# Retention's queries and its normalised output transposed by VectorE and GpSimd in place of TensorE

## The chip, the cores and the metric

The kernel runs on one core of a Trainium2 chip. The metric is the device time of one execution in microseconds. The engines are TensorE (PE in the rows; PEld is its weight load), VectorE (DVE), ScalarE (ACT), GpSimd (POOL) and SyncE (SP). Each works through its own queue in order, and they wait for one another on semaphores.

## The reference

Two blocks of layers on 256 tokens of width 1024, all in fp32: a SwiGLU feed-forward part, token mixing, a second feed-forward part, then a recurrent mixer and a short-convolution mixer. The change is in token mixing, and there in the retention branch (4 heads, queries and keys of 128, values of 256):

```python
rq, rk, rv, rg, nq, nk, nv, g_ret, g_na = jnp.split(u @ w_in, points, axis=-1)
q = _rotary(heads(rq, RET_QK_DIM), pos)
k = _rotary(heads(rk, RET_QK_DIM), pos) * (RET_QK_DIM ** -0.5)
y = _bidirectional_retention(q, k, heads(rv, RET_V_DIM), decay_fwd, decay_bwd)
y = y * lax.rsqrt(jnp.mean(y * y, axis=-1, keepdims=True) + RMS_EPS)
y_ret = (jax.nn.silu(rg) * y) @ w_ret_out
y_na = _neighborhood_attention(na_heads(nq), na_heads(nk), na_heads(nv), rel_bias) @ w_na_out
merged = jax.nn.sigmoid(g_ret) * y_ret + jax.nn.sigmoid(g_na) * y_na
return merged @ w_out
```

## The kernel before

Weights come as groups of 128x2048 numbers (1 MB) through a ring of six slots. SyncE asks for a group (L406) when TensorE has done with the group six before it. ScalarE rounds a group to its high part w_hi (L525, `round_to`), VectorE takes the rest as w_lo (L979, `low_to`), and a product of two fp32 matrices becomes three products of parts (L1610 to L1612). Activations are split in the same way and have to lie transposed, with the inner dimension on the partitions.

The mixing stage's input product goes by column blocks c = 0 to 12 and halves t = 0, 1 of the tokens. A step is called a slot: slot = 2c + t. Each engine has a loop over the slots, and after the product of a slot TensorE does small work from elsewhere (`extras`): in the slots 7 to 24 neighbourhood attention, where unit s has its scores in slot 7 + s, the transpose of its probabilities one slot later (L1828, waiting for VectorE's scaling L1232) and the product with the values two slots later (L1838). Retention runs between:

- slots 2 and 3: VectorE's `rotate` of rq, whose two parts GpSimd adds in `stage` (L489); slots 8 and 9 the same for rk;
- slots 6 and 7: TensorE transposes rq out of `stage` into PSUM (L1796), and VectorE copies it to rqT (L1197); slots 10 and 11 the same for rk;
- slots 12 to 15: scores of retention; slots 18 to 21: their product with the values, multiplied into the gate in y_ret (L1321);
- slot 22: ScalarE's root (L766), then VectorE's reciprocal and eight scalings of y_ret (L1331); behind these, at the head of slot 23, the scaling of the last unit's probabilities (L1231, L1232);
- slots 24 and 25: TensorE transposes y_ret (L1796), ScalarE takes the high part yretT_hi (L535) and VectorE the low part yretT_lo (L1007).

GpSimd also adds the mask to the attention biases (`mask_bias`, L479), a unit ahead of need at most two, each behind VectorE's reduction of an earlier unit, and loads them (L448). Then come the output products: na_out (2 groups) into acc, ret_out (4 groups) into aux, the merge on VectorE (L1344, L1353, L1355), mix_out. In the queues of ScalarE and VectorE the roundings of ret_out's groups 1 to 3 and of mix_out's first stand behind slot 25.

In the two feed-forward stages the hidden values are already transposed without TensorE: VectorE turns 32x32 blocks (L1139), and GpSimd carries the blocks between groups of 32 partitions with sixteen transfers for each pair of tiles (L459, `move_tiles`).

Of the kernel before, what the change touches and what calls it, by code (L numbers as in the profile page):

```python
# [63 lines left out]
for _name in ACC_READERS:  # L64
# [3 lines left out]
FILL_COUNTS = [("t1", 4), ("rq", 2), ("rk", 2), ("rs", 4), ("rp", 4),  # L68
               ("yret", 4), ("merged", 4), ("t2", 4), ("t3", 4),
# [3 lines left out]
SPLIT_COUNTS = [("t1", 4), ("yret", 4), ("merged", 4), ("t2", 4), ("t3", 4), ("gate", 6), ("t4", 4), ("b_in", 12)]  # L73
# [51 lines left out]
def build(nc, first_in, weights, x_turned_in, x_in, gain0_in, gains, rot_in, colmask_in, dist_in, decay_in, lam_in, bias_in, gate_w_in,  # L125
          gate_b_in, conv_a_in, conv_ab_in, conv_b_in, out):
    with ExitStack() as ctx:
# [77 lines left out]
        yretT_lo = at("yretT_lo", [P, KD, S], F32R, area + 24576)  # L205
        rqT = at("rqT", [P, RH, S], F32, area + 16384)
        rkT = at("rkT", [P, RH, S], F32, area + 20480)
        m_ret = at("m_ret", [P, T, DM], F32, area + 16384)
# [111 lines left out]
        y_ret_ready = sem("y_ret_ready")  # L320
        ret_acc_full = sem("ret_acc_full")
# [97 lines left out]
        def _(pool):  # L419
# [52 lines left out]

            def mask_bias(s):
                pool.wait_ge(bias_in_s[s % 2], 16 * (s // 2 + 1))
                if s == 0:
                    pool.wait_ge(consts_in, 16 * 8)
                if s >= 2:
                    pool.wait_ge(s_reduced, s - 1)
                g.tensor_tensor(bias_m[:, s % 2], bias_raw[:, s % 2],  # L479
                                colmask[:, KINDS[s % NB]].unsqueeze(1).to_broadcast([P, GR, KB]), ALU.add).then_inc(bias_ready, 1)  # L480
                if s + 2 < UNITS:
                    load_bias(s + 2)
# [3 lines left out]
            for n in range(2 * T):  # L486
                t = n % T
                pool.wait_ge(acc_free_dve[t], ACC_ORDER[:FIRST_ACC["mix_in"] + (2, 5)[n // T]].count("V"))
                g.tensor_tensor(stage[:, t], stage[:, t], rot_b[:, t], ALU.add).then_inc(rot_done, 1)  # L489
                if n:  # L490
                    mask_bias(n + 1)
            for s in range(2 * T + 1, UNITS):
                mask_bias(s)
            pool.wait_ge(bank_full, FIRST_FILL["rp"] + RH)
            load_gains(2, 3, 4)
            pool.wait_ge(xn_ready, 12)
# [20 lines left out]
        def _(act):  # L517
# [208 lines left out]
            for c in range(13):  # L726
                for t in range(T):
# [40 lines left out]
                    if slot in (24, 25):  # L768
                        tt = slot - 24
                        for h in range(2):  # L770
                            bank = h
                            take_hi("yret", 2 * tt + h, yretT_hi[:, 4 * h:4 * h + 4, tt * P:(tt + 1) * P], bank,
                                    source=aux[:, bank].rearrange("p (c q) -> p c q", c=4))
# [197 lines left out]
        def _(dve):  # L971
# [243 lines left out]
            for c in range(13):  # L1215
                for t in range(T):
# [21 lines left out]
                    if slot in (3, 8, 9):  # L1238
                        dve.wait_ge(acc_full[t], c0 + c + 1)
                        if c == 4:  # L1240
                            dve.wait_ge(bank_full, FIRST_FILL["rq"] + t + 1)
                        rotate(t, par, T * (c // 4) + t)
# [34 lines left out]
                    if slot in (6, 7, 10, 11):  # L1277
                        name, dst = ("rq", rqT) if slot < 10 else ("rk", rkT)
                        copy_fill(name, t, [(dst[:, :, t * P:(t + 1) * P], heads_of(0))])
# [53 lines left out]
                    if slot in (24, 25):  # L1333
                        tt = slot - 24
                        cols = slice(tt * P, (tt + 1) * P)
                        for h in range(2):
                            chunks = slice(4 * h, 4 * h + 4)
                            take_lo("yret", 2 * tt + h, yretT_lo[:, chunks, cols], yretT_hi[:, chunks, cols],
                                    heads_of(h))
            low_to(FIRST_GROUP["ret_out"] + 4)  # L1340
            for t in range(T):
                dve.wait_ge(acc_full[t], FIRST_ACC["na_out"] + 1)
                dve.wait_ge(acc_free_act[t], ACC_ORDER[:FIRST_ACC["na_out"]].count("A"))
                v.scalar_tensor_tensor(m_na[:, t], m_na[:, t], 1.0, acc[:, t].rearrange("p h n -> p (h n)"),  # L1344
                                       ALU.add, ALU.mult).then_inc(acc_free_dve[t], 1)
# [257 lines left out]
        def _(pe):  # L1603
# [237 lines left out]
            def extras(slot):  # L1841
                if slot in (6, 7, 10, 11):
                    t = slot % 2
                    n = slot - 6 if slot < 10 else slot - 8
                    pe.wait_ge(rot_done, n + 1)
                    transposes(0, stage[:, t], FIRST_FILL["rq"] + n)
                if 12 <= slot < 16:
                    h = slot - 12
                    pe.wait_ge(bank_free, FIRST_FILL["rs"] + h)
                    for k in range(T):  # L1850
# [25 lines left out]
                if slot in (24, 25):  # L1876
                    t = slot - 24
                    pe.wait_ge(y_ret_ready, t + 1)
                    for h in range(2):
                        transposes(h, y_ret[:, t, h * 512:(h + 1) * 512],  # L1880
                                   FIRST_FILL["yret"] + 2 * t)
# [33 lines left out]
            pe.wait_ge(bank_free, FIRST_FILL["yret"] + 4)  # L1915
            for t in range(T):
                for n in range(4):
# [229 lines left out]
```

## Time and profile before

| | us |
|---|---|
| median of 3 runs | 883.44 (883.14 to 883.91) |
| the profiled execution | 883.76 |
| its span | 882.0 |
| TensorE busy | 873.6 |
| VectorE busy | 602.2 |
| ScalarE busy | 461.9 |
| GpSimd busy | 174.5 |

The span runs from the first instruction to the last; the rest of an execution's time lies around it. Starts are microseconds from the span's start. TensorE's instructions are pipelined: the distance between two starts tells what one costs, the duration is longer. The mixing stage's slots lie from about 200 to 354, na_out begins at 354.49 and ret_out at 365.75.

### The profile page before, as it was taken

How to read it: one execution, taken by the hardware profiler on the slowest of the kernel's cores; microseconds unless marked ns; L12 is line 12 of the kernel's file. 1: busy time of each engine (PE TensorE's matmuls, PEld its weight loads, DVE VectorE, ACT ScalarE, POOL GpSimd, SP SyncE). 2: the span in 40 equal slices, each digit the busy share in tenths (PEclk: the TensorE clock that was granted, in tenths of full speed). 3: DMA queues.
4: the chain of work that ended last, by engine and by line, in shares of the span. 5: the costliest groups of instructions: out<-in, count | busy, mean ns of one | idle time of the engine just before them, and what ended most of it. 6: DMA issues, size and time to landing. Idle time of an engine off the chain costs nothing.

```text
span 882.0 us, 10831 instructions
## 1 busy us (share of the span) xinstructions
PE 873.6 (99%) x4320; PEld 737.3 (84%) x4320; DVE 602.2 (68%) x720; ACT 461.9 (52%) x570; POOL 174.5 (20%) x281
## 2 busy tenths in 40 slices
PE   9999999999999999999999999999999999999997
PEld 7788888888888888888888888888999888888886
DVE  6757666468767656577666667446979857888872
ACT  6645454455444556446444445445886644555551
POOL 2544452003021110000244445000480000000000
PEclk9999999999999999999999999999999999999999
DMA  9976665456653444455666666556434456555521
GB/s 348 367 232 228 215 219 211 143 191 203 260 202 133 172 174 171 185 191 190 246 216 216 215 216 224 192 203 247 162 128 159 169 187 241 191 191 191 191 96 48
DMA packets 33089, 175.62 MB, mean 199 GB/s; under 512 B 6688, under 2 KB 7248, under 8 KB 14096
## 3 DMA queue, kind: packets, MB, share of 16 engines
q1 hardware_dynamic: 24368, 161.23, 50.4%
q0 software_dynamic: 8384, 13.44, 5.1%
q8 instruction: 34, 0.56, 0.3%
q10 hardware_dynamic: 288, 0.27, 0.1%
q14 instruction: 15, 0.12, 0.0%
HBM read 167.05 MB, written 1.05 MB: 191 GB/s over the span
## 4 chain that ended last, share of the span: by engine, by line
PE 94%; DVE 2%; ACT 2%; DMA 1%; SPq 1%; issue 0%; ACTq 0%; DVEq 0%
PE acc L1610 22%; PE acc L1612 22%; PE acc L1611 22%; PE acc L2025 8%; PE acc L2027 4%; PE acc L1807 2%; PE acc L1977 2%; PE acc L1978 2%; PE acc L1976 2%; DMA raw<-weights 1%; DVE w_lo L979 1%; PE aux L1961 1%; PE aux L1728 1%; PE acc L1809 1%; PE aux L1611 1%; PE aux L1610 1%
## 5 line engine op out<-in xcount | busy, mean ns | idle before, releaser
L979 DVE TENSOR_TENSOR w_lo<-raw,w_hi 128x2048 fp32r<-128x2048 f32 x147 | 337.2, 2301 | 119.8 <-ACT w_hi L525 119.4
L525 ACT ACTIVATE w_hi<-raw 128x2048 fp32r<-128x2048 f32 x145 | 276.1, 1913 | 58.9 <-DMA raw<-weights 58.7
L1610 PE MATMUL acc<-w_hi,xT 128*128 128x512 f32 x600 | 236.2, 394 | 0.6 <-DVE w_lo L979 0.6
L1612 PE MATMUL acc<-w_hi,xT 128*128 128x512 f32 x600 | 233.8, 390 | 0.0
L1611 PE MATMUL acc<-w_lo,xT 128*128 128x512 f32 x600 | 233.6, 389 | 0.0
L459 POOL DMA_DIRECT2D hT_raw<-turned x192 | 109.6, 579 | 122.0 <-DVE turned L1139 120.3
L1610 PEld LDWEIGHTS acc<-w_hi,xT 128*128 128x128 f32 x600 | 112.7, 188 | 24.4 <-DVE w_lo L979 1.0
L1612 PEld LDWEIGHTS acc<-w_hi,xT 128*128 128x128 f32 x600 | 112.6, 188 | 23.8
L1611 PEld LDWEIGHTS acc<-w_lo,xT 128*128 128x128 f32 x600 | 112.7, 188 | 22.6
L2025 PE MATMUL acc<-xT,w_hi 128*128 128x512 f32 x320 | 111.3, 394 | 0.0
L2027 PE MATMUL acc<-xT,w_lo 128*128 128x256 f32 x320 | 88.7, 277 | 0.0
L2025 PEld LDWEIGHTS acc<-xT,w_hi 128*128 128x128 f32 x320 | 60.0, 188 | 13.8
L1610 PE MATMUL acc<-w_hi,hT_hi 128*128 128x512 f32 x176 | 68.6, 390 | 0.0
L1612 PE MATMUL acc<-w_hi,hT_lo 128*128 128x512 f32 x176 | 68.5, 389 | 0.0
L1611 PE MATMUL acc<-w_lo,hT_hi 128*128 128x512 f32 x176 | 68.5, 389 | 0.0
L2027 PEld LDWEIGHTS acc<-xT,w_lo 128*128 128x128 f32 x320 | 60.1, 188 | 0.0
L1128 DVE TENSOR_TENSOR prod<-acc,silu_g 128x256 f32<-128x256 f32 x44 | 18.6, 423 | 40.6 <-ACT silu_g L651 22.8
L651 ACT ACTIVATE silu_g<-acc 128x256 f32<-128x256 f32 x22 | 8.5, 385 | 60.5 <-PE acc L1612 60.0
L1612 PEld LDWEIGHTS acc<-w_hi,hT_lo 128*128 128x128 f32 x176 | 33.0, 188 | 6.9
L1611 PEld LDWEIGHTS acc<-w_lo,hT_hi 128*128 128x128 f32 x176 | 33.0, 188 | 6.8
L1610 PEld LDWEIGHTS acc<-w_hi,hT_hi 128*128 128x128 f32 x176 | 33.0, 188 | 6.8
L1610 PE MATMUL acc<-w_hi,yT_hi 128*128 128x512 f32 x96 | 37.5, 390 | 0.0
(244 smaller groups left out, 1144.3 us busy)
## 6 DMA issues: line engine op xcount, KB each, us to landing
raw<-weights SPq DMA_DIRECT2D x147, 1024.0 KB, 4.8
hT_raw<-turned POOLq DMA_DIRECT2D x160, 32.0 KB, 2.7
gain_pre<-gains POOLq DMA_DIRECT2D x5, 512.0 KB, 5.2
raw<-weights SPq DMA_DIRECT2D x4, 512.0 KB, 7.9
gain_post<-gains POOLq DMA_DIRECT2D x3, 512.0 KB, 5.9
gate_w<-gate_w_in POOLq DMA_DIRECT2D x1, 1536.0 KB, 9.1
x_turned<-x_turned_in SPq DMA_DIRECT2D x4, 256.0 KB, 5.1
x<-x_in SPq DMA_DIRECT2D x2, 512.0 KB, 12.1
```

The lines of the kernel that those rows point to most:

```text
L459: pool.dma_start(hT_raw[quad, chunks[0]:chunks[1], :, i, :].rearrange("p c t b -> p (c t) b"), turned[32 * i:32 * i + 32, p % 2, 0:n, :, q, :]
L525: a.activation(w_hi[:, g % RING], raw[:, g % RING], ACT.Copy).then_inc(hi_done, 1)
L979: v.tensor_tensor(w_lo[:, slot], raw[:, slot], w_hi[:, slot].bitcast(F32), ALU.subtract)\
L1128: v.tensor_tensor(prod[:, par, :, t], acc[:, t, par, 256:512].rearrange("p (c n) -> p c n", c=2), silu_g[:, t].rearrange("p (c n) -> p c n ...
L1610: m.matmul(dst, hi[:, k, cols], w_hi[:, slot, w], start=first, stop=False)
L1611: m.matmul(dst, hi[:, k, cols], w_lo[:, slot, w], start=False, stop=False)
L1612: return m.matmul(dst, lo[:, k, cols], w_hi[:, slot, w], start=False, stop=last)
L1807: m.matmul(dst, w_hi[:, g % RING, w], xT[:, k].rearrange("p a q -> p (a q)"), start=k == 0, stop=False)
L1976: m.matmul(dst, w_hi[:, slot, w], xT_hi[:, k, :], start=k == 0, stop=False)
L1977: m.matmul(dst, w_hi[:, slot, w], xT_lo[:, k, :], start=False, stop=False)
L2025: m.matmul(dst, w_hi[:, g % RING, w], xT[:, k].rearrange("p a q -> p (a q)"), start=k == 0, stop=False)
L2027: i = m.matmul(dst[:, 0:S], w_lo[:, g % RING, w], xT[:, k, 0], start=False, stop=k == KD - 1)
```

## The change

rq and y_ret are no longer transposed on TensorE. For each, VectorE turns the 32x32 blocks in place of the transposes (two instructions for rq in slots 4 and 5, two of 128x1024 for y_ret in slot 22), and GpSimd moves the blocks across partitions with sixteen transfers each (32 KB each for rq, 64 KB each for y_ret). rq lands in rqT directly; y_ret lands in yr_moved, from where ScalarE takes the high part and VectorE the low part, in two instructions of 128x1024 each, after slot 25. VectorE waits for rq's moves in slot 10 (rk's tile lies where rq_turned lay), TensorE in slot 12. TensorE's wait ahead of ret_out is for yretT_lo, one half of the tokens at a time. The declarations of the new semaphores are left out here.

```diff
@@ FILL_COUNTS, SPLIT_COUNTS
-FILL_COUNTS = [("t1", 4), ("rq", 2), ("rk", 2), ("rs", 4), ("rp", 4),
-               ("yret", 4), ("merged", 4), ("t2", 4), ("t3", 4),
+FILL_COUNTS = [("t1", 4), ("rk", 2), ("rs", 4), ("rp", 4),
+               ("merged", 4), ("t2", 4), ("t3", 4),
...
-SPLIT_COUNTS = [("t1", 4), ("yret", 4), ("merged", 4), ("t2", 4), ("t3", 4), ("gate", 6), ("t4", 4), ("b_in", 12)]
+SPLIT_COUNTS = [("t1", 4), ("merged", 4), ("t2", 4), ("t3", 4), ("gate", 6), ("t4", 4), ("b_in", 12)]
@@ tiles
+        yr_turned = at("yr_turned", [P, KD, T, QUADS, 32], F32, area + 53248)
+        yr_moved = at("yr_moved", [P, KD, T, QUADS, 32], F32, area + 24576)
+        rq_turned = at("rq_turned", [P, RH, T, QUADS, 32], F32, area + 20480)
+        rq_moved = rqT[:].rearrange("p h (t i b) -> p h t i b", t=T, b=32)
@@ GpSimd
+            def move_blocks(dst, src, done):
+
+                for i in range(QUADS):
+                    for q in range(QUADS):
+                        pool.dma_start(dst[32 * q:32 * q + 32, :, :, i, :].rearrange("p c t b -> p (c t) b"),
+                                       src[32 * i:32 * i + 32, :, :, q, :].rearrange("p c t b -> p (c t) b"))\
+                            .then_inc(done, 16)
...
                 if n:
                     mask_bias(n + 1)
+                if n == 1:
+                    pool.wait_ge(rq_tiles_turned, T)
+                    move_blocks(rq_moved, rq_turned, rq_landed)
             for s in range(2 * T + 1, UNITS):
                 mask_bias(s)
             pool.wait_ge(bank_full, FIRST_FILL["rp"] + RH)
             load_gains(2, 3, 4)
+            pool.wait_ge(yr_tiles_turned, T)
+            move_blocks(yr_moved, yr_turned, yr_landed)
@@ ScalarE
-                    if slot in (24, 25):
-                        tt = slot - 24
-                        for h in range(2):
-                            bank = h
-                            take_hi("yret", 2 * tt + h, yretT_hi[:, 4 * h:4 * h + 4, tt * P:(tt + 1) * P], bank,
-                                    source=aux[:, bank].rearrange("p (c q) -> p c q", c=4))
+            act.wait_ge(yr_landed, 16 * MOVES)
+            for t in range(T):
+                a.activation(yretT_hi[:, :, t * P:(t + 1) * P], yr_moved[:, :, t].rearrange("p c i b -> p c (i b)"),
+                             ACT.Copy).then_inc(yr_hi, 1)
             round_to(FIRST_GROUP["mix_out"] + 1)
@@ VectorE
-                        if c == 4:
-                            dve.wait_ge(bank_full, FIRST_FILL["rq"] + t + 1)
                         rotate(t, par, T * (c // 4) + t)
...
-                    if slot in (6, 7, 10, 11):
-                        name, dst = ("rq", rqT) if slot < 10 else ("rk", rkT)
-                        copy_fill(name, t, [(dst[:, :, t * P:(t + 1) * P], heads_of(0))])
+                    if slot in (4, 5):
+                        dve.wait_ge(rot_done, t + 1)
+                        v.transpose(rq_turned[:, :, t].rearrange("p c q b -> p c (q b)"),
+                                    stage[:, t].rearrange("p (c n) -> p c n", c=RH)).then_inc(rq_tiles_turned, 1)
+                    if slot in (10, 11):
+                        if t == 0:
+                            dve.wait_ge(rq_landed, 16 * MOVES)
+                        copy_fill("rk", t, [(rkT[:, :, t * P:(t + 1) * P], heads_of(0))])
...
                             i.then_inc(y_ret_ready, 1)
-                    if slot in (24, 25):
-                        tt = slot - 24
-                        cols = slice(tt * P, (tt + 1) * P)
-                        for h in range(2):
-                            chunks = slice(4 * h, 4 * h + 4)
-                            take_lo("yret", 2 * tt + h, yretT_lo[:, chunks, cols], yretT_hi[:, chunks, cols],
-                                    heads_of(h))
+                        for tt in range(T):
+                            dve.wait_ge(y_ret_ready, tt + 1)
+                            v.transpose(yr_turned[:, :, tt].rearrange("p c q b -> p c (q b)"),
+                                        y_ret[:, tt].rearrange("p (c n) -> p c n", c=KD)).then_inc(yr_tiles_turned, 1)
             low_to(FIRST_GROUP["ret_out"] + 4)
+            for t in range(T):
+                dve.wait_ge(yr_hi, t + 1)
+                cols = slice(t * P, (t + 1) * P)
+                v.tensor_tensor(yretT_lo[:, :, cols], yr_moved[:, :, t].rearrange("p c i b -> p c (i b)"),
+                                yretT_hi[:, :, cols].bitcast(F32), ALU.subtract).then_inc(yr_lo, 1)
@@ TensorE
-                if slot in (6, 7, 10, 11):
+                if slot in (10, 11):
                     t = slot % 2
-                    n = slot - 6 if slot < 10 else slot - 8
-                    pe.wait_ge(rot_done, n + 1)
-                    transposes(0, stage[:, t], FIRST_FILL["rq"] + n)
+                    pe.wait_ge(rot_done, T + t + 1)
+                    transposes(0, stage[:, t], FIRST_FILL["rk"] + t)
                 if 12 <= slot < 16:
                     h = slot - 12
                     pe.wait_ge(bank_free, FIRST_FILL["rs"] + h)
+                    if h == 0:
+                        pe.wait_ge(rq_landed, 16 * MOVES)
...
-                if slot in (24, 25):
-                    t = slot - 24
-                    pe.wait_ge(y_ret_ready, t + 1)
-                    for h in range(2):
-                        transposes(h, y_ret[:, t, h * 512:(h + 1) * 512],
-                                   FIRST_FILL["yret"] + 2 * t)
...
-            pe.wait_ge(bank_free, FIRST_FILL["yret"] + 4)
             for t in range(T):
+                pe.wait_ge(yr_lo, t + 1)
                 for n in range(4):
                     out_tile("ret_out", n, t, yretT_hi, yretT_lo, KD, aux_target, lambda t: (ret_acc_full, 1))
```

## Rows read from the trace of the kernel before

**Rows 1.** The page's busy time, share of the span and instructions of each engine.
```profile
PE 873.6 (99%) x4320; PEld 737.3 (84%) x4320; DVE 602.2 (68%) x720; ACT 461.9 (52%) x570; POOL 174.5 (20%) x281
```

**Rows 2.** The page's chain that ended last: shares of the span by engine.
```profile
PE 94%; DVE 2%; ACT 2%; DMA 1%; SPq 1%; issue 0%; ACTq 0%; DVEq 0%
```

**Rows 3.** Timeline of TensorE, slot 7: start, duration, engine, line, operation, out<-in, shape, count.
```profile
234.61 0.60 PE L1796 MATMUL aux<-ident,stage 128*128 128x128 f32 x4
235.05 0.39 PE L1821 MATMUL aux<-nkT,nqT 128*128 128x128 f32 x2
```

**Rows 4.** Timeline of TensorE from slot 23 to the start of ret_out.
```profile
341.21 0.33 PE L1828 MATMUL aux<-ident,prob 128*128 128x128 f32 x1
341.38 0.39 PE L1838 MATMUL aux<-probT,nv_b 128*128 128x128 f32 x2
341.52 0.48 PE L1610 MATMUL acc<-w_hi,xT 128*128 128x512 f32 x1
...
347.11 0.39 PE L1838 MATMUL aux<-probT,nv_b 128*128 128x128 f32 x2
...
348.12 0.47 PE L1610 MATMUL acc<-w_hi,xT 128*128 128x512 f32 x1
...
353.69 1.04 PE L1796 MATMUL aux<-ident,y_ret 128*128 128x128 f32 x8
354.49 0.47 PE L1610 MATMUL acc<-w_hi,ynaT_hi 128*128 128x512 f32 x1
...
365.75 0.40 PE L1610 MATMUL aux<-w_hi,yretT_hi 128*128 128x512 f32 x1
```

**Rows 5.** Timeline of VectorE, end of slot 22 and head of slot 23.
```profile
338.57 2.19 DVE L1331 TENSOR_SCALAR y_ret<-y_ret,ret_rstd 128x256 f32<-128x256 f32 x8
340.68 0.16 DVE L1231 RECIPROCAL prob_rec<-prob_sum 128x1 f32<-128x1 f32 x1
```

**Rows 6.** The feed-forward turns, whole span: durations in ns min/median/max, first and last start.
```profile
L1139 DVE STREAM_TRANSPOSE turned<-prod x22: 711/711/715, 28.9 to 534.1; 128x512 f32<-128x512 f32 x22
```

**Rows 7.** Feed-forward moves: turn before, two sets of sixteen, a weight request, two moves.
```profile
117.95 0.71 DVE L1139 STREAM_TRANSPOSE turned<-prod 128x512 f32<-128x512 f32 x1
...
L459 POOL DMA_DIRECT2D hT_raw<-turned x16: 584/584/584, 119.0 to 127.6; - x16
...
DMA to landing us min/median/max: 1.8/2.3/5.7
...
L459 POOL DMA_DIRECT2D hT_raw<-turned x16: 551/551/562, 129.8 to 138.0; - x16
...
125.06 0.33 SPq L406 DMA_DIRECT2D raw<-weights  x1
...
L459 POOL DMA_DIRECT2D hT_raw<-turned x2: 584/584/584, 124.7 to 125.3; - x2
...
DMA to landing us min/median/max: 3.1/4.1/5.2
```

**Rows 8.** Timelines of ScalarE and VectorE from the last slot to ret_out.
```profile
353.89 0.60 ACT L748 ACTIVATE m_na<-acc 128x512 f32<-128x512 f32 x1 [2.42 <-PE acc L1612]
354.39 1.08 ACT L535 ACTIVATE yretT_hi<-aux 128x512 fp32r<-128x512 f32 x2
355.34 5.53 ACT L525 ACTIVATE w_hi<-raw 128x2048 fp32r<-128x2048 f32 x3
...
357.31 6.70 DVE L979 TENSOR_TENSOR w_lo<-raw,w_hi 128x2048 fp32r<-128x2048 f32 x3 [1.00 <-ACT w_hi L525]
363.92 1.21 DVE L1344 SCALAR_TENSOR_TENSOR m_na<-m_na,acc 128x1024 f32<-128x1024 f32 x1
```

**Rows 9.** Timeline of SyncE's requests, last tile of the mixing input.
```profile
351.16 0.33 SPq L406 DMA_DIRECT2D raw<-weights  x1
```

**Rows 10.** Timelines of GpSimd and VectorE, slots 7 and 10.
```profile
236.93 0.46 POOL L479 TENSOR_TENSOR bias_m<-bias_raw,colmask 128x128 f32<-128x128 f32 x1 [19.68 <-DVE neg_max L1291]
...
254.75 0.68 DVE L1197 COPY rkT<-aux 128x512 f32<-128x512 f32 x1
```

More of the change, by code:

```diff
@@ L320, in build @@
         y_ret_ready = sem("y_ret_ready")
+        rq_tiles_turned, rq_landed = sem("rq_tiles_turned"), sem("rq_landed")
+        yr_tiles_turned, yr_landed = sem("yr_tiles_turned"), sem("yr_landed")
+        yr_hi, yr_lo = sem("yr_hi"), sem("yr_lo")
         ret_acc_full = sem("ret_acc_full")
```

## The prediction, made before the changed kernel was built

> **What bounds the kernel now.** I read the busy times first: TensorE is busy for 873.6 of 882.0 us [rows 1]. Then the chain of waits: 94% of the span is TensorE's own work [rows 2]. So time is won where TensorE loses instructions, and lost wherever it is made to wait; an engine with slack matters only at the place where TensorE asks for its result. Next I read TensorE's timeline at the transposes that go away [rows 3, 4], to price them by the distance between the starts of neighbouring instructions (one instruction's own duration overlaps the next). Then VectorE's timeline just before TensorE's wait in slot 23 [rows 5], because there the trace shows no slack at all: TensorE's transpose of the last probabilities starts at 341.21, 0.05 us after VectorE has scaled them (340.68, 0.53 us earlier, is where VectorE begins on that). Last, the moves that POOL already does in the feed-forward stages, as the model for the new ones [rows 7], and the run-up to ret_out [rows 8].
>
> **Removed from TensorE.** Four transposes for rq take 0.44 us (234.61 to 235.05), twice [rows 3]. In slot 24 the next tile starts 1.01 us after the last attend product (347.11 to 348.12); in slot 23, which has no y_ret transposes, 0.14 us (341.38 to 341.52): 0.87 us. In slot 25 eight transposes put 0.80 us ahead of na_out (353.69 to 354.49) [rows 4]. Sum: 0.44 + 0.44 + 0.87 + 0.80 = **2.55 us**, all on TensorE's path. If nothing else came of it, the time would fall by that.
>
> **rq's new way, costed at nothing.** VectorE turns stage in slots 4 and 5 (0.71 us each [rows 6]) and saves the two rqT copies out of PSUM in slots 6 and 7. POOL reaches the sixteen moves only after mask_bias(2), which waits for the first score reduction and starts at 236.93 [rows 10]. Behind them in POOL's queue stand the addition for rk, mask_bias(3) and the bias load after it. One move has 32 KB, as in the feed-forward stages, where sixteen are issued in 9.2 us; from about 238 they are issued by 247 and, with the worst landing there (5.7 us [rows 7]), in place by 253. VectorE waits for them just before its copy of rk at 254.75 [rows 10], and TensorE two slots later. The rk addition of slot 8 is held to 247 but is needed in slot 10, some 6 us later. The cover is thus about 2 us at the worst; beyond it every microsecond of lateness holds VectorE in slot 10 and the attention chain after it.
>
> **Slot 23: a wait in place of the transposes.** The two transposes of y_ret come right behind the normalisation in VectorE's queue (L1331, 338.57), ahead of the scaling of the last probabilities (340.68) [rows 5]. No row has a transpose of 128x1024. The 128x512 one takes 0.711 us [rows 6]; the bounds are that number and its double, 0.71 to 1.42. A 128x1024 operation of another kind takes 1.21 us (L1344) [rows 8], so I take 1.25 us, and 2.50 for the two. Queued behind them are the scaling, w_lo of na_out and the copy of probT; TensorE waits for the scaling alone. Having had no slack, it waits **2.50 us**. Call E the end of these transposes, 340.68 + 2.50 = 343.18 on the old clock (the 0.88 us won earlier left out). This alone takes back what was removed.
>
> **The run-up to ret_out.** TensorE's side, with E as zero and steps from [rows 4]: the transpose in slot 23 at 0.53, first product of the next tile 0.31 later (341.21 to 341.52), that tile 5.59 (to 347.11), 0.14 to the last tile, that tile 5.57 (348.12 to 353.69): na_out starts at E + 12.14. na_out takes 11.26 us (354.49 to 365.75): TensorE is free for ret_out at **E + 23.40**.
>
> The data's side. ScalarE finishes m_na 0.70 us after the last tile (353.69 to 354.39) [rows 4, 8]: E + 12.84. If the moves have landed, it makes yretT_hi, twice as large per instruction as the 128x512 pair that took 0.95 us (354.39 to 355.34): 1.90 for both. Only then come the roundings of ret_out's groups 1 to 3, and in VectorE's queue their w_lo stand ahead of yretT_lo: 1.97 from the first rounding to the first w_lo (355.34 to 357.31), 6.61 for three (to 363.92), 1.21 for the first yretT_lo by L1344's row [rows 8]. That is 11.69 us from the start of yretT_hi, so ret_out could start at E + 24.53. TensorE waits **1.13 us even if the moves come in time**. Here the old kernel had the split of y_ret done by slot 25; now it is late next, with three w_lo ahead of it. Behind yretT_lo in VectorE's queue m_na and the merge wait, but they need ret_out's first result, 11 us on.
>
> When do the moves land? POOL starts them 0.3 us after VectorE's transpose (117.95 + 0.71 against 119.0) [rows 7]. Sixteen of 256 blocks of 128 bytes are spread over 8.6 us (119.0 to 127.6), 0.576 apart; of 128 blocks over 8.2, 0.545 apart [rows 7]. The new ones have 512 blocks each. By that slope they are 0.64 us apart (estimate), within bounds of 0.576 and, if time went with the blocks, 1.15. The last is then issued at E + 0.3 + 15 x 0.64 = E + 9.9. Without company a move lands in 1.8 us. But a weight group was asked for at 125.06, and the move issued at 125.3 took 5.2 us instead [rows 7]. Here SyncE asks for a group 3.04 us into the last tile (348.12 to 351.16) [rows 4, 9], which will be E + 6.57 + 3.04 = E + 9.61. The last move comes 0.3 us behind it, as in the row, and lands at E + 15.1. ScalarE, free since E + 12.84, starts 2.26 us late, and so does ret_out: TensorE waits 1.13 + 2.26 = **3.39 us**.
>
> The Trainium skill (DMA: Bandwidth & Descriptors, "Queues, rings and completion order") says that each DMA engine takes turns between its queues packet by packet. By that a move need not wait for a whole weight group; the rows disagree, 5.2 us against 1.8, and I go by the rows.
>
> **Sum.** -2.55 + 2.50 + 3.39 = +3.34 us. After ret_out's start all transfers and waits follow TensorE, so the shift stays. The profiled execution took 883.76 us (span 882.0): 887.1. The median of the runs is 0.3 us lower, so I say **886.8 us**.
>
> **Rivals.**
> First, the moves miss the weight group: not slower. If 512 blocks cost no more issue time than 256, the last move is issued at E + 8.9, 0.7 us ahead of the request; the row with 1.8 us shows such moves landing at once. It decides at a spacing of about 0.60 us. Then only the 1.13 us remain: -2.55 + 2.50 + 1.13 = +1.08, 884.5 us. For it: the margin is a third of a microsecond. Against it: spacing does grow with the blocks. The Trainium skill's rule of turns would give the same time even behind the group.
>
> Second, POOL is the bound: at 1.15 us apart the last move is issued at E + 17.5 and lands at E + 19.3; ret_out starts at E + 31.0, a wait of 7.6 us, 891.0 us in all. At 0.8 apart the moves run into the next weight group too, which gives about 889.7. Against it: a doubling of blocks cost 6% before.
>
> Third, everything is hidden: neither wait comes, and 2.55 us are won, 880.9 us. It needs VectorE to reach the probabilities in slot 23 in time, against the order in its queue, and transposes far below 0.7 us.
>
> Fourth, VectorE keeps POOL from writing its moves. If each cost six times its 0.576 us, the last would be issued near E + 52 and the time would rise by over 35 us, to about 920. Against it: in the feed-forward stages the sixteen keep their spacing while VectorE works beside them [rows 7]. The Trainium skill (SBUF — State Buffer) warns that VectorE's fast fp32 copies lock GpSimd out of a shared port, so that such transfers wait for their descriptors; here no such copy runs in that stretch, and no row shows the wait.
>
> **How the numbers follow.** Forecast 0.50, first rival 0.25, second 0.14, third 0.09, fourth 0.02. The range takes in the first rival, the forecast with the bounds of the transposes (1.1 down, 0.3 up) and of the landing (5.7 for 5.2), and the milder half of the second: 883.6 to 889.8 us. A measurement of this kernel can tell 0.2%, 1.8 us, from no change. Faster by more than that needs the third rival: 0.09. Within it lies the first, with a little from the forecast's lower edge: 0.26. Slower: 0.65.
>
> **What would show it.** Right: in slot 23 TensorE idle for 2.5 us until VectorE's scaling; two transposes of about 1.25 us ahead of it; sixteen moves some 0.64 us apart, the last landing 5 us after issue; ScalarE idle on them; TensorE idle for over 3 us at ret_out until VectorE's yretT_lo; no new wait at slots 10 and 12. Wrong: a first idle much shorter, because the transposes are cheaper; moves all landed before ScalarE asks (884.5); or moves a microsecond apart (891). A wait on rq's moves in slot 10 would be an addition that I don't expect.

## The result, and the profile after

Median of nine runs: 888.60 us (885.48 to 890.08), beside 883.51 us (883.14 to 883.91) for nine runs of the kernel before. The ratio, which is near that of the means (the medians alone give 1.0058), is 1.0047, with a 95% interval of 1.0034 to 1.0060: slower by about half a per cent. The nine times fall in two groups, four from 885.48 to 886.13 us and five from 888.60 to 890.08 us, with nothing between. The profiled execution is of the upper group: it took 888.88 us, its span is 887.1 us (before: 882.0), and all rows of this section are its own.

The page's first rows (span; busy time of each engine, share and instructions; the chain that ended last, by engine) answer [rows 1] and [rows 2].

```profile
span 887.1 us, 10809 instructions
PE 872.7 (98%) x4296; PEld 736.1 (83%) x4296; DVE 606.1 (68%) x720; ACT 462.0 (52%) x568; POOL 195.4 (22%) x313
PE 89%; DVE 3%; ACT 3%; DMA 2%; POOL 1%; issue 1%; SPq 1%; DVEq 0%; ACTq 0%
```

TensorE has 24 instructions fewer, as the diff says, yet its busy time fell by only 0.9 us, and its share of the chain fell from 94% to 89%: for some stretch that chain now runs through other engines. The timelines say where. VectorE at the end of slot 22 and TensorE in slot 23 (start, duration, engine, line, operation, out<-in, count, and in brackets the idle time before it and what ended that), against [rows 4] and [rows 5]:

```profile
337.46 2.19 DVE L1352 TENSOR_SCALAR y_ret<-y_ret,ret_rstd 128x256 f32<-128x256 f32 x8
339.57 2.36 DVE L1356 STREAM_TRANSPOSE yr_turned<-y_ret 128x1024 f32<-128x1024 f32 x2
341.86 0.12 DVE L1249 RECIPROCAL prob_rec<-prob_sum 128x1 f32<-128x1 f32 x1
...
342.35 0.33 PE L1851 MATMUL aux<-ident,prob 128*128 128x128 f32 x1 [2.20 <-DVE prob L1250]
```

The two transposes hold VectorE from 339.57 to 341.86, 2.29 us, and TensorE idles for 2.20 us until the scaling behind them. Next the stretch up to ret_out, as the chain of waits tells it (start, time, what):

```profile
339.65 2.29 DVE yr_turned L1356 x2
...
342.22 9.68 POOL yr_moved L484 x15
351.91 5.71 DMA yr_moved<-yr_turned
...
357.64 2.01 ACT yretT_hi L790 x2
359.65 1.81 ACT w_hi L545
...
361.49 3.65 DVE w_lo L997 x2
...
365.90 2.28 DVE w_lo L997
368.18 1.15 DVE yretT_lo L1362
```

This is one unbroken path through four engines: the turn, the moves one by one, the landing of the last, ScalarE's two halves, and then three w_lo ahead of yretT_lo. In [rows 8] yretT_hi began at 354.39, straight after m_na; here it begins at 357.64. Where the lateness of the moves sets in is told by the answer on the two issued just ahead of SyncE's request of 351.42:

```profile
L484 POOL DMA_DIRECT2D yr_moved<-yr_turned x2: 651/651/651, 350.6 to 351.3; - x2
...
DMA to landing us min/median/max: 2.1/4.0/5.9
```

The one issued 0.8 us ahead of the request landed in 2.1 us, the one issued 0.16 us ahead in 5.9. That one (at 357.1) and the last move (at 357.6) landed about when the weight group itself did, 5.9 us after its request (at 357.3).

TensorE's side of it, and the windows around it (columns: stretch and its length, then busy time and instructions of PE, PEld, DVE, ACT and POOL, granted clock, DMA share, GB/s):

```profile
351.42 0.33 SPq L413 DMA_DIRECT2D raw<-weights  x1
...
369.37 0.80 PE L1633 MATMUL aux<-w_hi,yretT_hi 128*128 128x512 f32 x1 [4.07 <-DVE yretT_lo L1362]
...
372.48 0.40 PE L1634 MATMUL aux<-w_lo,yretT_hi 128*128 128x512 f32 x1
```

```profile
365.20:369.30 4.10, 0.10 (x1) 0.00 (x0) 4.10 (x4) 1.91 (x1) 0.00 (x0) 0.96 0.96 372
369.30:372.40 3.10, 3.03 (x7) 2.46 (x8) 3.07 (x4) 0.00 (x0) 0.00 (x0) 0.50 0.05 21
372.40:376.00 3.60, 3.60 (x17) 2.96 (x17) 0.44 (x1) 0.00 (x0) 0.00 (x0) 1.00 0.00 0
```

TensorE idles for 4.07 us ahead of ret_out, and its granted clock then stands at 0.50, the lower of its two levels (1.2 GHz), until 372.4. Seven products take 3.11 us there (369.37 to 372.48); seven of the same line take 1.60 us at 1.00 (experiment weights_first, below: 366.95 to 368.55). That is 1.5 us more.

The account of this execution, in spans: -2.55 (instructions gone, as priced) + 2.20 (slot 23) + 4.07 (ret_out) + 1.5 (half clock after it) = +5.2 us; measured 887.1 - 882.0 = +5.1.

### The profile page after: what moved, and what is told of

It reads as the page before. It is cut to its first block, busy times and chain, and to the rows that moved or that the text cites. A ratio compares the mean times of both kernels' runs of the same rounds, so it can differ in the third digit from the quotient of the medians.

```text
span 887.1 us, 10809 instructions
## 1 busy us (share of the span) xinstructions
PE 872.7 (98%) x4296; PEld 736.1 (83%) x4296; DVE 606.1 (68%) x720; ACT 462.0 (52%) x568; POOL 195.4 (22%) x313
## 3 DMA queue, kind: packets, MB, share of 16 engines
HBM read 167.05 MB, written 1.05 MB: 189 GB/s over the span
## 4 chain that ended last, share of the span: by engine, by line
PE 89%; DVE 3%; ACT 3%; DMA 2%; POOL 1%; issue 1%; SPq 1%; DVEq 0%; ACTq 0%
PE acc L1633 21%; PE acc L1635 21%; PE acc L1634 21%; PE acc L2043 8%; PE acc L2045 4%; PE acc L1830 2%; DVE w_lo L997 2%; PE acc L1995 2%; PE acc L1996 2%; PE acc L1994 2%; DMA raw<-weights 1%; POOL yr_moved L484 1%; PE aux L1979 1%; PE aux L1633 1%; PE aux L1635 1%; PE aux L1634 1%
```

## The experiments

My theory: the removed instructions are worth their 2.55 us, and what is lost comes from two places in in-order queues, y_ret's transposes ahead of VectorE's scaling (slot 23) and the wait for the moves ahead of three roundings and splits (ret_out). The rivals were that the moves as such are too late, that the two waits add up independently, that the lateness isn't due to the weight request, and that a wait costs TensorE its length and no more. "Before" is the median of the kernel before in the same session.

**Weights first.** ScalarE rounds all groups of ret_out ahead of its wait for the moves:

```
+            round_to(FIRST_GROUP["ret_out"] + 4)
             act.wait_ge(yr_landed, 16 * MOVES)
```

> The changed kernel with one order altered: ScalarE rounds ret_out's groups 1 to 3 ahead of its wait for y_ret's moves, so that behind the moves only one high part and one low part stand (0.95 + 1.2 us instead of 11.7). Theory (ret_out is held by moves that land behind a weight group, and then by the three w_lo queued ahead of yretT_lo): TensorE's 4.07 us of idle time before ret_out shrinks below 1 us, the granted clock no longer falls there, slot 23 keeps its 2.2 us; the time comes to about the time of the kernel before, 883 to 884 us. Rival (the moves themselves are too late): idle of at least 2 us stays before ret_out and the time stays above 885.5.

Measured: 884.47 us (882.88 to 885.35, 11 runs) against 883.44; ratio 1.0008, interval 0.9999 to 1.0017. The timeline of TensorE has no idle time left ahead of ret_out, while the wait in slot 23 is unchanged:

```profile
342.59 0.33 PE L1852 MATMUL aux<-ident,prob 128*128 128x128 f32 x1 [2.20 <-DVE prob L1251]
...
366.72 0.39 PE L1636 MATMUL acc<-w_hi,ynaT_lo 128*128 128x512 f32 x1
366.95 0.40 PE L1634 MATMUL aux<-w_hi,yretT_hi 128*128 128x512 f32 x1
...
368.55 0.39 PE L1635 MATMUL aux<-w_lo,yretT_hi 128*128 128x512 f32 x1
```

```profile
342.00:346.00 4.00, 3.41 (x11) 2.77 (x12) 3.96 (x6) 0.93 (x1) 3.54 (x6) 0.64 0.84 295
```

So the moves were early enough for ret_out; it was the order behind them that was late, three splits in front of yretT_lo. (In this execution SyncE's request came only at 353.23, behind the last move, and no move took over 3.1 us; last_group_after, below, has late moves and no wait either.) The window shows what I had not looked for: in this execution the granted clock fell already after slot 23's wait (a mean of 0.64 from 342 to 346, where the profile of the changed kernel has 1.00). The sum is -2.55 + 2.20 = -0.35 without that fall (883.1 us) and some 1.5 us more with it (884.6). The eleven times agree: four from 882.9 to 883.8 us, each with a granted clock of 0.999 in the mean of the whole execution, and seven from 884.3 to 885.4 us at 0.997 or 0.998.

**Probabilities first.** VectorE does the transposes in slot 23, behind the scaling that TensorE waits for, not in slot 22 ahead of it:

```
                             .then_inc(p_scaled, 1)
+                    if slot == 23:
+                        for tt in range(T):
+                            dve.wait_ge(y_ret_ready, tt + 1)
+                            v.transpose(yr_turned[:, :, tt]..., y_ret[:, tt]...).then_inc(yr_tiles_turned, 1)
```

> The changed kernel with one order altered: VectorE scales the last probabilities in slot 23 before it turns y_ret, so the wait in slot 23 goes. Theory (the chain from the turns over the moves sets ret_out's start, so the wait in slot 23 only comes out of a later one): slot 23's idle time of 2.2 us vanishes, TensorE asks for the weight groups 2 us earlier against the moves, the last of them land behind the second group, and the idle time before ret_out grows to 6 or 7 us: 888 to 890 us, no gain. Rival (the two waits add, as the sum had them): the time falls by 2.2 us against the changed kernel, to 886 or less.

Measured: 891.76 us (891.16 to 891.90, 4 runs) against 883.44; ratio 1.0092, interval 1.0079 to 1.0106. One wait is gone and the kernel is 3 us slower than with it. The answer on the sixteen moves, TensorE's timeline, and a window:

```profile
DMA to landing us min/median/max: 2.2/2.7/7.3
```

```profile
371.02 0.80 PE L1634 MATMUL aux<-w_hi,yretT_hi 128*128 128x512 f32 x1 [8.27 <-DVE yretT_lo L1363]
```

```profile
366.00:376.00 10.00, 4.98 (x12) 3.96 (x13) 8.46 (x6) 2.50 (x2) 0.00 (x0) 0.50 0.09 36
```

Without the wait TensorE reaches the tiles sooner, so SyncE asks for two weight groups before the moves are through (348.86 and 351.58), the last move lands 7.3 us after its issue, and TensorE idles for 8.27 us at ret_out. The whole window from 366 to 376 has the lower clock; the twelve products from 371.02 on take 5.29 us there instead of 12 x 0.23 = 2.8. Sum: -2.55 + 8.27 + 2.5 = +8.2; measured +7.9 in spans. The waits don't add up: what TensorE doesn't lose in slot 23 it loses at ret_out, and more. I expected 888 to 890; the idle time and the clock were both larger than I had them.

**Both orders.** The two edits together.

> Both alterations together: probabilities before the turns in slot 23, roundings before the wait for the moves. Theory: neither wait is left, what remains is the 2.55 us of removed transposes with at most 1 us of wait before ret_out: 881 to 882 us, faster than the kernel before. Rival (removed transposes are worth less than their spacing, or moves behind the second weight group still hold ret_out): 883 us or more.

Measured: 884.46 us (882.92 to 885.51, 11 runs) against 883.44; ratio 1.0008, interval 1.0000 to 1.0017. I had expected 881 to 882: a miss by 2.5 us or more. Slot 23 has no wait, but ret_out has one again, for another reason. First the timelines of SyncE, ScalarE, VectorE and TensorE, then the answer on the landing of that request:

```profile
351.24 0.33 SPq L413 DMA_DIRECT2D raw<-weights  x1
...
359.44 1.92 ACT L545 ACTIVATE w_hi<-raw 128x2048 fp32r<-128x2048 f32 x1 [2.99 <-DMA raw<-weights]
361.38 2.29 DVE L998 TENSOR_TENSOR w_lo<-raw,w_hi 128x2048 fp32r<-128x2048 f32 x1 [2.61 <-ACT w_hi L545]
...
364.87 0.50 PE L1635 MATMUL aux<-w_hi,yretT_hi 128*128 128x512 f32 x1 [2.46 <-DVE yretT_lo L1364]
```

```profile
DMA to landing us min/median/max: 8.2/8.2/8.2
```

The group asked for at 351.24 shares its time with the moves and lands 8.2 us later; ScalarE waits 2.99 us for it, and since all groups now stand ahead of yretT_hi, the late group holds what TensorE needs first. The delay goes both ways: the moves are late behind a group, and a group is late among the moves (in weights_first two groups, asked for 2.7 us apart like these but with all moves landed, took about 4.7 us each).

The profiled execution is the shortest of the eleven, 882.92 us. Its granted clock stays at 1.00 behind the wait of 2.46 us (364 to 370), and -2.55 + 2.46 = -0.1; its span, 0.8 us below that of before, is shorter still. Five of the eleven took 882.9 to 883.6 us at a mean clock of 0.999; six took 884.5 to 885.5 us, five of them at 0.996 or 0.997. A fall of the clock would account for the six, but none of them has a profile.

**The last group behind.** Both orders, but ScalarE rounds only up to ret_out's third group ahead of its wait, and VectorE's split of the fourth stands behind yretT_lo:

```
+            round_to(FIRST_GROUP["ret_out"] + 3)
             act.wait_ge(yr_landed, 16 * MOVES)
...
-            low_to(FIRST_GROUP["ret_out"] + 4)
+            low_to(FIRST_GROUP["ret_out"] + 3)
             for t in range(T):
                 dve.wait_ge(yr_hi, t + 1)
...
+            low_to(FIRST_GROUP["ret_out"] + 4)
```

> The two alterations together, and one more: ret_out's last weight group, which TensorE needs some 8 us after ret_out's start, is rounded by ScalarE behind yretT_hi and split by VectorE behind yretT_lo; the two groups before it stay ahead. Theory (what still held ret_out in the run with both orders was the last group, landed 8.2 us after its request and standing ahead of yretT_lo): the idle time of 2.46 us before ret_out goes, no fall of the granted clock is left in the mixing stage, and the 2.55 us of removed transposes show: 880.5 to 881.5 us in every run. Rival (the moves, which landed as late as 7.8 us after issue, are late by themselves): at least 1 us of idle time stays and some runs lose to the clock, 882.5 us or more.

Measured: 881.03 us (880.54 to 881.60, 9 runs) against 883.51; ratio 0.9973, interval 0.9963 to 0.9982. It beats both kernels, by 2.48 us the one before: the 2.55 us of the removed instructions, with both waits gone. The timelines of ScalarE, VectorE and TensorE, and the window behind slot 23:

```profile
360.03 2.01 ACT L791 ACTIVATE yretT_hi<-yr_moved 128x1024 fp32r<-128x1024 f32 x2 [2.67 <-DMA yr_moved<-yr_turned]
361.13 2.36 DVE L1364 TENSOR_TENSOR yretT_lo<-yr_moved,yretT_hi 128x1024 fp32r<-128x1024 f32 x2 [1.44 <-ACT yretT_hi L791]
363.88 2.29 DVE L998 TENSOR_TENSOR w_lo<-raw,w_hi 128x2048 fp32r<-128x2048 f32 x1 [0.39 <-ACT w_hi L545]
...
362.98 0.39 PE L1638 MATMUL acc<-w_hi,ynaT_lo 128*128 128x512 f32 x1
363.21 0.40 PE L1636 MATMUL aux<-w_hi,yretT_hi 128*128 128x512 f32 x1
```

```profile
342.00:346.00 4.00, 4.00 (x19) 3.31 (x18) 4.00 (x4) 1.04 (x1) 3.05 (x5) 1.00 0.84 294
```

The moves still land late (ScalarE waits 2.67 us for them), but now the wait stands where it holds nothing that TensorE asks for: ret_out follows na_out without a gap (362.98, 363.21).

**The request held back.** SyncE asks for ret_out's third group only when the moves have landed:

```
+                if g == FIRST_GROUP["ret_out"] + 2:
+                    sp.wait_ge(yr_landed, 16 * MOVES)
```

> The changed kernel, with SyncE's request for ret_out's third weight group held until y_ret's moves have landed. Theory (the runs near 888.8 us are those in which the last moves land behind that group): every move lands within about 3 us, the idle time before ret_out shrinks from 4.07 to about 2 us, and no run is near 888.8; all lie between 884 and 886.5 us. Rival (the two groups of times have another cause, such as the granted clock alone): runs near 888.8 us remain in about half of the cases.

Measured: 885.49 us (884.39 to 886.40, 11 runs) against 883.51; ratio 1.0020, interval 1.0011 to 1.0029. The answer on the moves (count, duration in ns, first and last issue, landing), and TensorE's timeline:

```profile
L486 POOL DMA_DIRECT2D yr_moved<-yr_turned x16: 648/650/691, 342.2 to 351.8; - x16
...
DMA to landing us min/median/max: 2.1/2.5/3.2
```

```profile
367.90 0.50 PE L1635 MATMUL aux<-w_hi,yretT_hi 128*128 128x512 f32 x1 [1.05 <-DVE yretT_lo L1364]
```

With the issue unchanged (about 0.65 us apart) the longest landing is 3.2 us instead of 5.7, the wait at ret_out 1.05 us instead of 4.07, and no run is near the upper group of the changed kernel. The profile alone doesn't decide it: in this execution the granted clock fell in slot 23 (a mean of 0.70 from 342 to 346), and that by itself makes the request late, as again_1 shows below. The times do: none of eleven is above 886.4 us, where five of nine were at 888.6 or more, and the four shortest (884.4 to 884.8) are near what -2.55 + 2.20 + 1.05 = +0.7 gives with no fall of the clock, 884.2. The group of weights asked for beside the moves is the cause of their lateness.

**The changed kernel again, three times.** Single profiles, to see what sets the two groups of times apart.

> The changed kernel as it is, to see a profile of each of its two groups of times. Theory: if the time is near 888.8 us, as in the first profile, the granted clock falls only after the wait ahead of ret_out and the last moves land over 5 us after issue; if it is near 886 us, the clock falls after the wait in slot 23, TensorE then asks for the weight group more than 1 us later, all moves land within about 3 us and the wait ahead of ret_out is about 1 us. Rival: the two groups differ in something else, and both show the late landing.

> The same kernel once more, with the same two expectations: late landing and a wait of about 4 us ahead of ret_out near 888.8 us; a fall of the clock in slot 23, landings within 3 us and a wait of about 1 us near 886 us.

> The same kernel a third time, with the same two expectations: late landing and a wait of about 4 us ahead of ret_out near 888.8 us; a fall of the clock in slot 23, landings within 3 us and a wait of about 1 us near 886 us.

Measured: 886.65, 890.50 and 889.47 us (before: 883.17). The first belongs with the lower group, though 0.5 us above its longest. Its timelines (slot 23, SyncE's request, ret_out), the window behind slot 23, and the answer on the moves:

```profile
342.85 0.37 PE L1851 MATMUL aux<-ident,prob 128*128 128x128 f32 x1 [2.19 <-DVE prob L1250]
...
353.50 0.33 SPq L413 DMA_DIRECT2D raw<-weights  x1
...
368.43 0.50 PE L1633 MATMUL aux<-w_hi,yretT_hi 128*128 128x512 f32 x1 [1.05 <-DVE yretT_lo L1362]
```

```profile
342.00:346.00 4.00, 3.15 (x9) 2.58 (x10) 3.96 (x6) 1.20 (x1) 3.28 (x6) 0.62 0.89 313
```

```profile
DMA to landing us min/median/max: 2.1/2.3/3.1
```

After slot 23's wait the granted clock fell. TensorE took some 1.6 us longer for the tile behind it (its slot 23 stands 0.50 us later than in the first profile, its request 2.08 us later), so SyncE's request came when the last move was already issued: landing 3.1 us at most, a wait of 1.05 us at ret_out, and no second fall. The two of the upper group had the request at 351.62 and 351.10, landings of 5.9 and 5.7 us, waits of 4.16 and 3.81 us, and the lower clock behind ret_out. The execution in which TensorE ran slower behind slot 23 took 2.8 to 3.9 us less than these two.

**Idle time alone.** In the kernel before, TensorE waits ahead of ret_out for an empty step of VectorE behind m_na, in the second version behind two more operations of 128x1024 (their results unused):

```
+            for n in range(0):      # second version: range(2)
+                step(v.scalar_tensor_tensor(rot_b[:]..., x[:, 1], 1.0, x[:, 1], ALU.add, ALU.mult))
+            dve.wait_ge(acc_free_dve[1], ...)
+            v.memset(spare2[:], 0.0).then_inc(idle_over, 1)
...
+            pe.wait_ge(idle_over, 1)
```

> The kernel before, with TensorE made to wait ahead of ret_out until VectorE has finished m_na's second half: about 1.6 us of idle time and nothing else. Theory (idle time costs its length, and beyond a certain length also a fall of the granted clock): about 885.0 us, granted clock unchanged at 1.00 around 370 us. Rival (any idle time brings the clock down): 886.4 us or more.

> The same with two more operations of VectorE of some 1.25 us each in front of TensorE: about 4.1 us of idle time, as long as the changed kernel's wait ahead of ret_out. Theory: 4.1 us and a fall of the granted clock to half for some 3 us after TensorE resumes, worth 1.5 us: about 889.0 us. Rival (the lower clock belongs to the changed kernel's other work, not to the idle time): 887.5 us, granted clock 1.00.

Measured: 885.12 us (884.48 to 885.36, 10 runs; ratio 1.0018, interval 1.0009 to 1.0027) and 890.24 us (889.40 to 890.44, 4 runs; ratio 1.0075, interval 1.0061 to 1.0088), against 883.51. TensorE's timeline and a window, of the first:

```profile
366.90 0.47 PE L1617 MATMUL aux<-w_hi,yretT_hi 128*128 128x512 f32 x1 [1.49 <-issue]
```

```profile
370.00:373.00 3.00, 3.00 (x15) 2.49 (x14) 0.00 (x0) 0.00 (x0) 0.00 (x0) 1.00 0.00 0
```

and the same two views of the second:

```profile
369.36 0.77 PE L1617 MATMUL aux<-w_hi,yretT_hi 128*128 128x512 f32 x1 [3.88 <-issue]
```

```profile
370.00:373.00 3.00, 3.00 (x9) 2.35 (x8) 0.00 (x0) 0.00 (x0) 0.00 (x0) 0.50 0.02 5
```

1.49 us of idle time cost 1.6; 3.88 us cost 6.7, 2.8 more than its length: at half clock nine products were done from 370 to 373 instead of fifteen. I had 889.0 for the second, with the clock's share too small. Nothing here moves data or changes an order of transfers, so a wait does cost TensorE more than its length.

**rq alone.** Only rq's part of the diff on the kernel before (the turn in slots 4 and 5, POOL's moves, the two waits; rq's transposes out of slots 6 and 7).

> Only rq goes the new way; y_ret is transposed by TensorE as before. Theory: two groups of four transposes leave TensorE's path and nothing takes their place: 0.9 us less than the kernel before, 882.6 us. Rival (the rq moves disturb the weight stream or VectorE in slot 10): no gain or a loss, 883.5 us or more.

Measured: 882.75 us (882.38 to 882.91, 11 runs) against 883.44; ratio 0.9991, interval 0.9982 to 1.0000. The answer on the moves, and VectorE's timeline at its copy of rk:

```profile
L480 POOL DMA_DIRECT2D rqT<-rq_turned x16: 582/582/609, 237.1 to 245.8; - x16
...
DMA to landing us min/median/max: 1.8/2.2/6.1
```

```profile
254.65 0.68 DVE L1211 COPY rkT<-aux 128x512 f32<-128x512 f32 x1
```

The last move is in place by 252 at the latest (245.8 + 6.1) and the copy starts without a wait. VectorE did not get it for nothing, though:

```profile
250.23 1.40 DVE L1246 TENSOR_SCALAR prob<-prob,prob_rec 128x128 f32<-128x128 f32 x1
```

GpSimd's two additions for rk are held up by the moves. The first (from 246.36) now falls beside a w_lo, and the addition takes 2.54 us instead of 1.28, the w_lo 3.31 instead of 2.29; the second (from 250.22) falls beside this scaling, which took 0.29 us before. VectorE's idle time ahead of the next w_lo went from 1.32 us to 0.21. It had that much slack, so TensorE did not wait.

The median is 0.69 us lower; two groups of transposes were priced at 0.88.

## Why the prediction was right, and where it was not

**Removed from TensorE: 2.55 us.** Right. last_group_after, where both waits are gone, is 2.48 us faster than before, and rq_only shows its share.

**rq at nothing.** Right for TensorE: no wait at VectorE's copy of rk, with some 2.6 us of cover (254.65 against 252) where I had about 2. That GpSimd's late additions would lengthen VectorE's operations by some 2 us in all was not on my list; VectorE's slack took it up (rq_only).

**Slot 23: 2.50 us.** Right in place and cause; the size was 2.20, since one transpose of 128x1024 takes 1.15 us and not 1.25.

**Ret_out: 3.39 us, of which 2.26 from the late moves.** The steps came out as worked, with E, the end of the transposes, at 341.86:

| step | predicted | measured |
|---|---|---|
| distance of moves | 0.64 us | 0.65 us |
| last move issued | E + 9.9 | 351.91: E + 10.05 |
| SyncE's request | E + 9.61 | 351.42: E + 9.56 |
| last move landed | E + 15.1 | 357.62: E + 15.76 |
| yretT_hi to ret_out | 11.69 us | 357.64 to 369.37: 11.73 us |
| TensorE free | E + 23.40 | 369.37 - 4.07 = 365.30: E + 23.44 |
| wait | 3.39 us | 4.07 us |

The mis-sized term is the landing: 5.7 us, where I took the 5.2 of one row. (The other 0.15 us is the issue, E + 10.05 for E + 9.9.) [rows 7] has 5.7 as its longest, and I used that only as the bound. The Trainium skill (DMA: Bandwidth & Descriptors, "Queues, rings and completion order") has each DMA engine take turns between its queues packet by packet. These runs don't show the moves gaining by that: they took 5.7 us beside a 1 MB group and landed about when it did, and 3.2 us at the longest when the group's request was held back.

**Left out: the clock.** This is the step that failed. The sum counted each wait of TensorE at its length; -2.55 + 2.20 + 4.07 gives +3.7, and the profile has +5.1. The 1.4 us between them are the products at half clock behind ret_out's wait (1.5 us, above), and idle_long shows the same with nothing else changed. Such a term could not be worked out from the rows of before that I had read, but a bound for it should have been there, since both waits were forecast; I put it at nothing without a reason. The Trainium skill (TensorE: Matmul & The Clock Gate, "Part 1: The HAM clock gate") says that the chip lowers TensorE's clock by how busy it has been of late; the rows agree (0.50 behind the wait, 1.00 from 372.4 on).

**One value for two.** The forecast of 886.8 us lies in the gap between the two groups. That it is near both is in part luck: the clock was not in the sum, and had one of the five upper runs fallen into the lower group, the median would have been about 886. The upper group is the forecast's mechanism plus the clock: 888.6 to 890.1. The lower group has the first rival's mechanism (the moves miss the weight group; the wait at ret_out is 1.05 us, where I gave 1.13), but for a reason I did not have: the clock falls in slot 23 and delays the request past the last move. -2.55 + 2.20 + 1.6 + 1.05 = +2.3, about 885.8 us; measured 885.5 to 886.1. (again_1 itself, at 886.65, stood 0.50 us later than the first profile before either wait.) My 884.5 for that rival lacked the clock again; hold_request, with the moves clear of the group, had times from 884.4 on.

**The other rivals.** POOL as the bound is out (0.65 us apart, not 0.8 or 1.15), and VectorE did not hold back POOL's issue. (That last rival was priced too low: by the sum's own steps E + 52 makes a wait of some 42 us, about 925 and not 920.) "All hidden" at 880.9 did not come about in the kernel as changed, but its price was right: last_group_after is that case, at 881.03.

**Direction.** Slower, by more than a measurement can tell, as forecast at 0.65. For the upper group that is plain (+5.1 to +6.6 us); the lower one (+2.0 to +2.6) is only just past 1.8 us.

## What to carry to other kernels

Work taken off the bounding engine brings its time only if the replacement stands, in every in-order queue that it passes through, behind the things which that engine asks for sooner: here two re-orderings and one split moved behind turned +5.1 us into -2.5 without one instruction less. Cost a wait of the bounding engine at more than its length when it is some microseconds long, since its clock may be at half for a while after. Before a wait is taken away, ask which transfer request it was holding back.

## What the runs showed of the hardware

**Small moves and a large load delay one another.** A move of 64 KB between partitions landed in 2.1 us by itself, in 5.7 issued 0.5 us behind the request for a 1 MB group, in 5.9 issued 0.16 us ahead of it (all three in the first profile of the changed kernel), and in 7.3 with two groups under way (probs_first). Beside one group it landed about when the group did. A group took about 4.7 us with no move under way (weights_first), 5.9 beside the last two moves, and 8.2 as the second of two among the moves (both_orders).

**GpSimd and VectorE beside one another.** In rq_only an addition of GpSimd's and a w_lo of VectorE's that overlap took 2.54 and 3.31 us, where apart they took 1.28 and 2.29 in the kernel before. The sixteen issues of moves beside VectorE's work kept their 0.58 us.

**A wait and the granted clock.** After 1.05 and 1.49 us of idle time no fall was seen (hold_request, again_1, idle_short). After waits of about 2.2 us in slot 23 the clock fell in three profiles (weights_first, hold_request, again_1) and not in three others (the first of the changed kernel, again_2, again_3), although four of the six are the same kernel; nor did it after 2.46 us ahead of ret_out (the profile of both_orders). After 3.8 to 8.3 us it fell every time, and seven products or more then ran at 0.50. What decides at 2.2 to 2.5 us stays open.

**One kernel, two times.** The two groups, some 3 us apart, come from this, as far as four profiles show it: whether the clock falls in one wait decides whether the last moves are out well ahead of a transfer's request or beside it. again_1 stands against again_2, again_3 and the first profile for it; the nine timed runs, but for the profiled one, have no profile, and are put down to it by their times alone.
